# A trunk of four normalised sub-layers on one core: VectorE adds the squares of the first feed-forward's entry norms, token blocks 0 and 1

## The chip, the cores and the metric

The kernel runs on one core of a Trainium2 chip. The metric is the device time of one execution in microseconds (us), lower is better. The program is one launch that computes every output of the reference.

## The reference

One step of a two-layer trunk over 1024 prompt tokens and 8 x 16 sample tokens (1152 tokens together), model width 1024. Each layer is a mixer and a gated feed-forward, with an RMS norm before and after each:

```
def rms_norm(x, g):
    xf = x.astype(jnp.float32)
    y = xf * lax.rsqrt(jnp.mean(xf * xf, axis=-1, keepdims=True) + NORM_EPS)
    return (y * g.astype(jnp.float32)).astype(x.dtype)
...
        x = x + rms_norm(mix, g[1])
        f, fb = conv_ffn(rms_norm(x, g[2]), f_conv[layer], w['ffn_w_up'][layer], w['ffn_conv_w'][layer],
                         w['ffn_conv_b'][layer], w['ffn_w_down'][layer])
```

The case is about layer 0, between its mixer and its feed-forward: the mixer ends with `out = ag[..., :D_MODEL] * sigmoid(ag[..., D_MODEL:])` with `ag = z @ w_glu`, and then come the two norms above, `rms_norm(mix, g[1])` and `rms_norm(x, g[2])`.

## The kernel before

Features lie on the 128 partitions, in 8 tiles (`KD` = 8); the 1152 tokens lie along the free axis, in 3 blocks of 384 (`NB` = 3, `TB` = 384).

**The GLU steps.** `front` runs 24 steps, numbered k, block c = k // 8 and output tile m = k % 8. `Glu.tensor` computes in each step two halves, h = 0 (the gate) and h = 1 (the value), of 24 products of 128x384: a weight is split into a rounded head and the rest, and head times head, head times rest and rest times head are added (`products`). I call such a half a unit, numbered 2k + h. The weights of unit n are loaded by the SP queue into `w_raw` (`Weights.load`, which waits until the split of unit n - 2 is done), rounded by ScalarE into `w_head` (`Weights.round`, L836, which waits for the load and until TensorE is done with unit n - 2), and subtracted by VectorE into `w_rest` (`Weights.subtract`, L840). TensorE starts unit n when both are done. ScalarE then forms the sigmoid (L1617) and VectorE the product with it (L1623), which goes into `f`.

**The norms.** `Norm` handles six groups g = 0 to 5, two for each token block: group 2c is the norm of `f` for block c, group 2c + 1 the norm of x + norm(f). While the GLU steps of blocks 1 and 2 run, the groups 0 to 3 of blocks 0 and 1 run between them. In steps with m = 0 (even groups) and m = 4 (odd groups) ScalarE squares the block pair by pair, each pair 128x768 (two feature tiles), into three buffers `sq` (`Norm.squares`, L1423). The sum over the 1024 features is made by TensorE after the step with m = 1 or m = 5 (`Norm.sums`, L1433): for each of the four pairs, two tiles by three token columns of 128, six products of 128x128 with a matrix of ones, so 24 a group. ScalarE takes the root (`roots`, L1441), VectorE the inverse and widens it (`inverse`), TensorE spreads it over the partitions after the next step (`spread`, L1457), and VectorE scales (`scale`, L1486, and the addition to x, L1482) in the steps m = 2 and 3, or 6 and 7. As there are three buffers and four pairs, the fourth square has to wait until the first pair has been summed; ScalarE's program has it in the step m = 1 or 5:

```
                for h in range(2):
                    if c and m in (0, 4):
                        norm1.squares(act, g + m // 4, 2 * h, h + 2, glu.free, KD * (c - 1))
                    if c and m in (1, 5) and h == 1:
                        norm1.squares(act, g + m // 4, 3, 4, glu.free, KD * (c - 1))
                    if c and m == 7:
                        norm1.heads(act, c - 1, 2 * h, 2 * h + 2)
                    w.round(act, 2 * k + 2 + h, h)
```

Groups 4 and 5 (block 2) come after the last GLU step, among the first units of the feed-forward. GpSimd issues the loads and stores of x (its own DMA queue) and computes `x_rest` of blocks 0 and 1 (`Norm.rest`, L1462).

The order of each engine's instructions is that of the written program; nothing is scheduled by costs. Between engines only semaphores order the work. Buffer numbers in the names (`sq_182`) are those of the built program.

Of the kernel before, what the change touches and what calls it, by code (L numbers as in the profile page):

```python
# [20 lines left out]
P = 128  # L21
D = 1024
KD = D // P
# [1355 lines left out]
class Norm:  # L1379


    def __init__(self, env, f, x_dram, post, pre, h_head, h_rest, x, sq, wide, small):
# [7 lines left out]
        self.scaled, self.renewed, self.headed = (sem(n) for n in ("scaled", "renewed", "headed"))  # L1390

    TT, HALF = TB // P, KD // 2
# [18 lines left out]
    def squares(self, act, g, k0, k1, ready=None, at=0):  # L1411

        c, r = self.place(g)
        for k in range(k0, k1):
            n = self.HALF * g + k
            if n >= 3:
                act.wait_ge(self.summed, n - 2)
            if r == 1:
                act.wait_ge(self.renewed, self.HALF * c + k + 1)
            else:  # L1420
                act.wait_ge(ready, at + 2 * k + 2)
            src = self.pair(self.f, k, c) if r == 0 else self.x[c][:, 2 * k:2 * k + 2, :]
            act.activation(self.sq[n % 3][:, :, :], src, ACT.Square).then_inc(self.squared, 1)  # L1423

    def sums(self, pe, g):
        for k in range(self.HALF):
            n = self.HALF * g + k
            pe.wait_ge(self.squared, n + 1)
            if g and k == 0:
                pe.wait_ge(self.rooted, g)  # L1430
            for h in range(2):
                for j in range(self.TT):
                    m = pe.matmul(self.env.bank[6][:, P * j:P * j + P], self.sq[n % 3][:, h, P * j:P * j + P], self.env.ones[:, :],  # L1433
                                  start=(k == 0 and h == 0 and j == 0), stop=(k == self.HALF - 1 and h == 1), skip_group_check=True)
            m.then_inc(self.summed, 1)

    def roots(self, act, g):
        act.wait_ge(self.summed, self.HALF * g + self.HALF)
        if g >= 2:
# [622 lines left out]
def front(env, i, x_head, x_rest, x_res, m_par, gates, tails, m_tails, xm_d, xc_d, sz_d):  # L2062
# [20 lines left out]
    norm1 = Norm(env, f, x_res, 1, 2, x_head, x_rest, [xs[0], xs[1], xs[0]], [two(f"sq{k}", A0 + 24576 + 3072 * k) for k in range(3)],  # L2083
                 wides(A0 + 33792), small)
    ys = [big("y_even", A1), big("y_odd", U0)]
# [14 lines left out]
    with nc.Block() as block:  # L2100
# [124 lines left out]
        def _(act):  # L2225
            w.round(act, 0, 0, first=True)
            w.round(act, 1, 1, first=True)
            for k in range(steps):
# [1333 lines left out]
```

## Time and profile before

| what | value |
|---|---|
| time, median of 3 runs | 3905.59 us (3903.67 to 3906.49) |
| the profiled execution | span 3903.4 us; its own time is not listed apart from the three above |
| instructions of the span | 53745 |
| TensorE busy | 3481.6 us, 89% of the span |
| VectorE busy | 1908.1 us, 49% |
| ScalarE busy | 1149.8 us, 29% |
| GpSimd busy | 511.1 us, 13% |
| mean granted TensorE clock | 0.935 of full |
| GLU steps 8 to 23, during which groups 0 to 3 run | about 360.8 to 524.4 us of the span |

The span runs from the first to the last instruction, the time is that of the whole execution. PE is TensorE, PEld its weight load, DVE VectorE, ACT ScalarE, POOL GpSimd. A PE instruction's duration reaches from its start to its end in the pipeline, so that the durations of consecutive ones overlap; what one costs is seen in the distance between two starts. A product of two float32 operands with the ones stands in the trace as two PE instructions (48 for the 24 products of a group). "<-issue" ahead of a PE instruction means that the profile shows no other engine that released it at that time.

### The profile page before, as it was taken

The numbers are of one execution on the slowest core, as the hardware profiler recorded it, in microseconds if no ns is written. First come the engines' busy times: TensorE is split into PE (matmuls) and PEld (weight loads), VectorE is DVE, ScalarE is ACT, GpSimd is POOL, SyncE is SP. The second block draws the span as 40 slices with busy tenths as digits, with TensorE's granted clock in tenths as the row PEclk, the third lists the DMA queues.
The fourth block names the chain that finished last, engine by engine and source line by source line (L and its number), as shares of the span: only waits on it lengthen the run. The fifth ranks groups of instructions, "written<-read, shape, count | busy, mean of one in ns | idle before, by whom it ended". The sixth has DMA issues, their size and how long they took to land. (4 is left out here: it accounts for less than half of the span.)

```text
span 3903.4 us, 53745 instructions
## 1 busy us (share of the span) xinstructions
PE 3481.6 (89%) x20489; PEld 3262.9 (84%) x20489; DVE 1908.1 (49%) x2953; ACT 1149.8 (29%) x1880; POOL 511.1 (13%) x769
## 2 busy tenths in 40 slices
PE   5549989999999989999478779997995999999997
PEld 4449989999999989999344468887985999999996
DVE  8933554445444563222533346664655544454455
ACT  5233343332333232222222212222112323323321
POOL 2240111000000120000120032221001100000000
PEclk8679999999999999999678789998997999999998
DMA  3444431111111123332399632222122111111112
GB/s 78 140 121 137 134 96 44 39 44 44 39 44 44 57 101 120 106 104 94 84 262 297 214 92 81 75 67 76 38 71 75 44 39 44 44 41 42 44 38 101
DMA packets 366303, 337.08 MB, mean 86 GB/s; under 512 B 42888, under 2 KB 294024, under 8 KB 365956
## 3 DMA queue, kind: packets, MB, share of 16 engines
q1 hardware_dynamic: 345318, 288.49, 24.1%
q0 software_dynamic: 13600, 38.24, 3.7%
q10 hardware_dynamic: 7176, 7.35, 0.6%
q8 instruction: 157, 2.57, 0.3%
q14 instruction: 52, 0.43, 0.0%
HBM read 231.12 MB, written 100.53 MB: 85 GB/s over the span
## 5 line engine op out<-in xcount | busy, mean ns | idle before, releaser
L1583 PE MATMUL pair<-x_head,w_head 128*128 128x384 f32 x1488 | 505.6, 340 | 53.0 <-DVE w_rest L840 30.4
L1583 PE MATMUL pair<-x_rest,w_head 128*128 128x384 f32 x1488 | 502.5, 338 | 0.0
L1583 PE MATMUL pair<-x_head,w_rest 128*128 128x384 f32 x1488 | 502.1, 337 | 0.0
L840 DVE TENSOR_TENSOR w_rest<-w_raw,w_head 128x1024 fp32r<-128x1024 f32 x228 | 291.9, 1281 | 414.4 <-ACT w_head L836 414.3
L836 ACT ACTIVATE w_head<-w_raw 128x1024 fp32r<-128x1024 f32 x228 | 242.4, 1063 | 686.8 <-PE pair L856 166.9
L1238 PE MATMUL pair<-x_head,w_head 128*128 128x384 f32 x1056 | 354.0, 335 | 10.5 <-DVE w_rest L840 7.5
L1238 PE MATMUL pair<-x_rest,w_head 128*128 128x384 f32 x1056 | 353.5, 335 | 0.0
L1238 PE MATMUL pair<-x_head,w_rest 128*128 128x384 f32 x1056 | 353.5, 335 | 0.0
L1583 PEld LDWEIGHTS pair<-x_head,w_head 128*128 128x128 f32 x1488 | 283.5, 191 | 58.0 <-issue 52.5
L1328 DVE SCALAR_TENSOR_TENSOR cv<-u,par,cv 128x1024 f32<-128x1024 f32 x88 | 112.8, 1282 | 358.5 <-ACT u L1294 358.5
L1583 PEld LDWEIGHTS pair<-x_rest,w_head 128*128 128x128 f32 x1488 | 283.5, 191 | 0.0
L1583 PEld LDWEIGHTS pair<-x_head,w_rest 128*128 128x128 f32 x1488 | 283.3, 190 | 0.0
L1851 DVE SCALAR_TENSOR_TENSOR cv<-u,par,cv 128x1024 f32<-128x1024 f32 x88 | 112.8, 1282 | 340.4 <-ACT u L1792 340.4
L1238 PEld LDWEIGHTS pair<-x_head,w_head 128*128 128x128 f32 x1056 | 198.9, 188 | 11.5 <-issue 7.5
L1238 PEld LDWEIGHTS pair<-x_rest,w_head 128*128 128x128 f32 x1056 | 198.8, 188 | 0.0
L1238 PEld LDWEIGHTS pair<-x_head,w_rest 128*128 128x128 f32 x1056 | 198.8, 188 | 0.0
L1753 PE MATMUL pair<-a_head,w_head 128*128 128x384 f32 x528 | 179.9, 341 | 2.2 <-DVE f L1882 0.9
L1289 ACT ACTIVATE cv<-pair,par 128x384 f32<-128x384 f32 x132 | 88.5, 670 | 315.5 <-PE pair L1238 304.5
L1259 PE MATMUL pair<-a_head,w_head 128*128 128x384 f32 x528 | 179.3, 340 | 1.5 <-DVE f L1355 0.4
L1753 PE MATMUL pair<-a_rest,w_head 128*128 128x384 f32 x528 | 177.5, 336 | 0.0
L1753 PE MATMUL pair<-a_head,w_rest 128*128 128x384 f32 x528 | 177.5, 336 | 0.0
L1259 PE MATMUL pair<-a_head,w_rest 128*128 128x384 f32 x528 | 177.5, 336 | 0.0
(510 smaller groups left out, 6982.0 us busy)
## 6 DMA issues: line engine op xcount, KB each, us to landing
w_raw<-in_ffn_w_up_dram SPq DMA_DIRECT2D x88, 512.0 KB, 3.9
hs<-in_state_mlstm_C_dram SPq DMA_DIRECT2D x52, 512.0 KB, 6.6
out_dram<-hs SPq DMA_DIRECT2D x52, 512.0 KB, 4.5
w_raw<-in_s_w_glu_dram SPq DMA_DIRECT2D x48, 512.0 KB, 4.1
w_raw<-in_ffn_w_down_dram SPq DMA_DIRECT2D x44, 512.0 KB, 3.7
w_raw<-in_mlstm_w_up_dram SPq DMA_DIRECT2D x32, 512.0 KB, 4.3
xm_d<-xm SPq DMA_DIRECT2D x16, 576.0 KB, 3.9
xc_d<-xc SPq DMA_DIRECT2D x16, 576.0 KB, 2.8
```

The source lines that it names most:

```text
L836: act.activation(self.head[slot][:, :], self.raw[slot][:, :], ACT.Copy).then_inc(self.rounded, 1)
L840: dve.tensor_tensor(self.rest[slot][:, :], self.raw[slot][:, :], self.head[slot][:, :].bitcast(F32), ALU.subtract).then_inc(self.split, 1)
L1238: m = pe.matmul(banks[k % 2][c][:, 0:TB], lhs[k % 2][:, P * i:P * i + P], rhs[:, i, TB * c:TB * c + TB], start=(i == 0 and q == 0), stop=( ...
L1259: ins = pe.matmul(banks[m % 2][c][:, 0:TB], lhs[m // 4][:, cols], rhs[s][:, k, TB * c:TB * c + TB], start=(k == 0 and q == 0), stop=(k == ...
L1289: act.activation(cv[g][:, TB * c:TB * c + TB], bk[c][:, 0:TB], ACT.Identity, scale=at(par, t, TAP + H, TAP + H + 1), bias=at(par, t, BIAS, ...
L1328: ins = dve.scalar_tensor_tensor(out=cp, in0=up[:, j:j + SEQ], scalar=tw, in1=cp, op0=ALU.mult, op1=ALU.add)
L1583: m = pe.matmul(out[:, 0:TB], lhs[slot][:, P * k:P * k + P], rhs[:, k, TB * c:TB * c + TB], start=(k == 0 and q == 0), stop=(k == KD - 1 a ...
L1753: ins = pe.matmul(out[:, 0:TB], lhs[m // 4][:, cols], rhs[s][:, k, TB * c:TB * c + TB], start=(k == 0 and q == 0), stop=(k == 1 and q == 2))
L1851: ins = dve.scalar_tensor_tensor(out=cp, in0=up[:, j:j + SEQ], scalar=tw, in1=cp, op0=ALU.mult, op1=ALU.add)
```

## The change

`Norm` gets an argument `gathers`, the number of groups handled in the new way; the first feed-forward's entry norms (`norm1`) get 4, so groups 0 to 3, and all other norms keep 0. In such a group VectorE adds the second, third and fourth square pair to the first (`gather`, three additions of 128x768), and TensorE multiplies only the sum with the ones: one pair, six products. All four squares now come in the step m = 0 or 4. The fourth goes into the buffer of the second, and therefore waits until VectorE has added the second.

```
+    def slot(self, g, k):
+        return self.sq[(g + (0, 1, 2, 1)[k]) % 3 if g < self.gathers else (self.HALF * g + k) % 3]
...
+    def gather(self, dve, g, k0, k1):
+        for k in range(k0, k1):
+            dve.wait_ge(self.squared, self.HALF * g + k + 1)
+            if k > 1:
+                dve.wait_ge(self.gathered, 3 * g + k - 1)
+            dve.tensor_tensor(self.slot(g, 0)[:, :, :], self.slot(g, 0)[:, :, :], self.slot(g, k)[:, :, :], ALU.add).then_inc(self.gathered, 1)
...
@@ squares @@
-            if n >= 3:
-                act.wait_ge(self.summed, n - 2)
+            if g < self.gathers:
+                if g and k == 0:
+                    act.wait_ge(self.gathered, 3 * g)
+                if g and k == 2:
+                    act.wait_ge(self.summed, g)
+                if k == 3:
+                    act.wait_ge(self.gathered, 3 * g + 1)
...
@@ sums @@
-        for k in range(self.HALF):
-            n = self.HALF * g + k
-            pe.wait_ge(self.squared, n + 1)
+        parts = (0,) if g < self.gathers else range(self.HALF)
+        for k in parts:
+            if g < self.gathers:
+                pe.wait_ge(self.gathered, 3 * g + 3)
...
@@ front, scalar @@
                     if c and m in (0, 4):
-                        norm1.squares(act, g + m // 4, 2 * h, h + 2, glu.free, KD * (c - 1))
-                    if c and m in (1, 5) and h == 1:
-                        norm1.squares(act, g + m // 4, 3, 4, glu.free, KD * (c - 1))
+                        norm1.squares(act, g + m // 4, 2 * h, 2 * h + 2, glu.free, KD * (c - 1))
...
@@ front, vector @@
+                if c and m in (1, 5):
+                    norm1.gather(dve, g + m // 4, 2, 4)
                 w.subtract(dve, 2 * k + 2, 0)
+                if c and m in (0, 4):
+                    norm1.gather(dve, g + m // 4, 1, 2)
```

How this stands in the programs. First ScalarE, steps 20 and 21 (block 2, m = 4 and 5, group 3), before: L1617 is the sigmoid, `w_head` the rounding of a unit's weights, `sq` a square, L1441 the root.

```order
L1617 ACTIVATE gate_170<-pair 128x384
L1423 ACTIVATE sq_182_2458<-x_odd_2457 128x768
L1423 ACTIVATE sq_183_2459<-x_odd_2457 128x768
L836 ACTIVATE w_head_150<-w_raw_148 128x1024
L1423 ACTIVATE sq_184_2460<-x_odd_2457 128x768
L836 ACTIVATE w_head_151<-w_raw_149 128x1024
L1617 ACTIVATE gate_171<-pair 128x384
L836 ACTIVATE w_head_150<-w_raw_148 128x1024
L1423 ACTIVATE sq_182_2458<-x_odd_2457 128x768
L836 ACTIVATE w_head_151<-w_raw_149 128x1024
L1441 ACT_TABLE_LOAD
```

The same place of the changed program.

```order
L1648 ACTIVATE gate_170<-pair 128x384
L1433 ACTIVATE sq_182_2458<-x_odd_2457 128x768
L1433 ACTIVATE sq_183_2459<-x_odd_2457 128x768
L836 ACTIVATE w_head_150<-w_raw_148 128x1024
L1433 ACTIVATE sq_184_2460<-x_odd_2457 128x768
L1433 ACTIVATE sq_183_2459<-x_odd_2457 128x768
L836 ACTIVATE w_head_151<-w_raw_149 128x1024
L1648 ACTIVATE gate_171<-pair 128x384
L836 ACTIVATE w_head_150<-w_raw_148 128x1024
L836 ACTIVATE w_head_151<-w_raw_149 128x1024
L1472 ACT_TABLE_LOAD
```

The fourth square has moved from the second step to the first, ahead of the rounding of the first step's second unit.

Next VectorE, steps 12 and 13 (block 1, m = 4 and 5, group 1), before: `w_rest` is the subtraction of a unit's weights, `f<-pair,gate` the product with the sigmoid, L1446 the inverse.

```order
L840 TENSOR_TENSOR w_rest_152<-w_raw_148,w_head_150 128x1024
L840 TENSOR_TENSOR w_rest_153<-w_raw_149,w_head_151 128x1024
L1623 TENSOR_TENSOR f<-pair,gate_170 128x384
L840 TENSOR_TENSOR w_rest_152<-w_raw_148,w_head_150 128x1024
L840 TENSOR_TENSOR w_rest_153<-w_raw_149,w_head_151 128x1024
L1623 TENSOR_TENSOR f<-pair,gate_171 128x384
L1446 RECIPROCAL small_166<-small_164 128x3
```

The same place of the changed program.

```order
L840 TENSOR_TENSOR w_rest_152<-w_raw_148,w_head_150 128x1024
L1451 TENSOR_TENSOR sq_183_2459<-sq_183_2459,sq_184_2460 128x768
L840 TENSOR_TENSOR w_rest_153<-w_raw_149,w_head_151 128x1024
L1654 TENSOR_TENSOR f<-pair,gate_170 128x384
L1451 TENSOR_TENSOR sq_183_2459<-sq_183_2459,sq_182_2458 128x768
L1451 TENSOR_TENSOR sq_183_2459<-sq_183_2459,sq_184_2460 128x768
L840 TENSOR_TENSOR w_rest_152<-w_raw_148,w_head_150 128x1024
L840 TENSOR_TENSOR w_rest_153<-w_raw_149,w_head_151 128x1024
L1654 TENSOR_TENSOR f<-pair,gate_171 128x384
L1477 RECIPROCAL small_166<-small_164 128x3
```

One addition (L1451) has come between the two subtractions of the first step, and two ahead of the first subtraction of the second.

## Rows read from the trace of the kernel before

**Rows 1.** The page: span, TensorE, and granted clock in 40 equal slices

```profile
span 3903.4 us, 53745 instructions
...
PE 3481.6 (89%) x20489; PEld 3262.9 (84%) x20489; DVE 1908.1 (49%) x2953; ACT 1149.8 (29%) x1880; POOL 511.1 (13%) x769
...
PEclk8679999999999999999678789998997999999998
```

**Rows 2.** Busy time by stretch, columns as in its first line

```profile
core 0: us, PE busy (x) PEld busy (x) DVE busy (x) ACT busy (x) POOL busy (x), PEclk, DMA share, GB/s
352.60:436.60 84.00, 83.37 (x516) 82.49 (x516) 38.25 (x53) 34.44 (x42) 5.71 (x8) 1.00 0.49 148
...
446.20:451.54 5.34, 0.01 (x1) 0.04 (x1) 5.34 (x2) 1.06 (x1) 4.14 (x3) 0.70 0.02 7
451.54:455.20 3.66, 3.66 (x12) 3.66 (x13) 1.50 (x2) 0.00 (x0) 0.74 (x1) 0.51 0.60 164
455.20:524.40 69.20, 68.83 (x434) 68.22 (x433) 29.85 (x40) 27.24 (x33) 4.36 (x6) 1.00 0.45 138
```

**Rows 3.** Waits, 352.6 to 524.4 us: total us, times, longest

```profile
PE pair L1583 <- issue: 6.8, 4, 5.3
...
ACT w_head L836 <- DMA w_raw<-in_s_w_glu_dram: 2.7, 1, 2.7
```

**Rows 4.** Timeline, PE, first sums: start, us, instruction

```profile
373.67 5.52 PE L1433 MATMUL pair<-ones,sq 128*128 128x128 f32 x48
378.95 0.42 PE L1583 MATMUL pair<-x_head,w_head 128*128 128x384 f32 x1
```

**Rows 5.** Busy time by stretch: sums of the second and fourth groups

```profile
413.62:418.89 5.27, 5.27 (x49) 5.27 (x49) 1.69 (x2) 3.07 (x3) 0.00 (x0) 1.00 0.34 97
...
501.55:506.82 5.27, 5.27 (x49) 5.27 (x49) 1.69 (x2) 3.07 (x3) 0.00 (x0) 1.00 0.33 98
```

**Rows 6.** Groups of instructions, 352.6 to 563 us

```profile
L1423 ACT ACTIVATE sq<-f 128x768 f32<-128x768 f32 x12 | 9.6, 836 | 12.1 <-PE pair L1433 12.1
...
L1482 DVE TENSOR_TENSOR x_even<-x_even,f 128x768 f32<-128x768 f32 x8 | 7.5, 954 | 0.0
```

**Rows 7.** Timeline, ACT, steps 8 and 9

```profile
360.98 0.49 ACT L1617 ACTIVATE gate<-pair 128x384 f32<-128x384 f32 x1 [3.07 <-PE pair L1583]
361.36 1.57 ACT L1423 ACTIVATE sq<-f 128x768 f32<-128x768 f32 x2
362.83 1.05 ACT L836 ACTIVATE w_head<-w_raw 128x1024 fp32r<-128x1024 f32 x1
363.78 0.84 ACT L1423 ACTIVATE sq<-f 128x768 f32<-128x768 f32 x1
365.20 1.06 ACT L836 ACTIVATE w_head<-w_raw 128x1024 fp32r<-128x1024 f32 x1 [0.58 <-PE pair L1583]
369.71 0.49 ACT L1617 ACTIVATE gate<-pair 128x384 f32<-128x384 f32 x1 [3.45 <-PE pair L1583]
...
375.21 0.84 ACT L1423 ACTIVATE sq<-f 128x768 f32<-128x768 f32 x1 [4.06 <-PE pair L1433]
```

**Rows 8.** Timeline, DVE, then PE, step 8

```profile
363.92 1.23 DVE L840 TENSOR_TENSOR w_rest<-w_raw,w_head 128x1024 fp32r<-128x1024 f32 x1 [4.28 <-ACT w_head L836]
...
364.76 0.34 PE L1583 MATMUL pair<-x_head,w_rest 128*128 128x384 f32 x1
365.24 0.41 PE L1583 MATMUL pair<-x_head,w_head 128*128 128x384 f32 x1
```

**Rows 9.** Timeline, DVE, POOL and PE, step 16

```profile
443.98 8.59 DVE L840 TENSOR_TENSOR w_rest<-w_raw,w_head 128x1024 fp32r<-128x1024 f32 x2 [1.82 <-ACT w_head L836]
...
443.19 7.15 POOL L1462 TENSOR_TENSOR x_rest<-f,x_head 128x768 fp32r<-128x768 f32 x4
...
451.54 0.66 PE L1583 MATMUL pair<-x_head,w_head 128*128 128x384 f32 x1 [5.34 <-issue]
```

**Rows 10.** DMA issues, 352 to 563 us: count, KB, us to landing

```profile
w_raw<-in_s_w_glu_dram SPq DMA_DIRECT2D x30, 512.0 KB, 4.0
```

More of the change, by code:

```diff
@@ L1379, with __init__ @@
 class Norm:
-    def __init__(self, env, f, x_dram, post, pre, h_head, h_rest, x, sq, wide, small):
+    def __init__(self, env, f, x_dram, post, pre, h_head, h_rest, x, sq, wide, small, gathers=0):
         self.env, self.f, self.x_dram, self.post, self.pre = env, f, x_dram, post, pre
@@ L1390, in __init__ @@
         self.scaled, self.renewed, self.headed = (sem(n) for n in ("scaled", "renewed", "headed"))
+        self.gathered, self.gathers = sem("gathered"), gathers
     TT, HALF = TB // P, KD // 2
@@ L1415, in squares @@
             n = self.HALF * g + k
-            if n >= 3:
-                act.wait_ge(self.summed, n - 2)
+            if g < self.gathers:
[5 more added lines that the diff above has]
+                    act.wait_ge(self.gathered, 3 * g + 1)
+            elif n >= 3:
+                if self.gathers:
+                    act.wait_ge(self.gathered, 3 * min(g, self.gathers))
+                act.wait_ge(self.summed, self.sums_of(g, k - 3) + 1)
             if r == 1:
@@ L1422, in squares, with sums_of @@
             src = self.pair(self.f, k, c) if r == 0 else self.x[c][:, 2 * k:2 * k + 2, :]
-            act.activation(self.sq[n % 3][:, :, :], src, ACT.Square).then_inc(self.squared, 1)
-    def sums(self, pe, g):
-        for k in range(self.HALF):
-            n = self.HALF * g + k
-            pe.wait_ge(self.squared, n + 1)
+            act.activation(self.slot(g, k)[:, :, :], src, ACT.Square).then_inc(self.squared, 1)
+    def slot(self, g, k):
+        return self.sq[(g + (0, 1, 2, 1)[k]) % 3 if g < self.gathers else (self.HALF * g + k) % 3]
+    def sums_of(self, g, k):
+        if k < 0:
+            g, k = g - 1, k + self.HALF
+        return g if g < self.gathers else self.gathers + self.HALF * (g - self.gathers) + k
+    def gather(self, dve, g, k0, k1):
[4 more added lines that the diff above has]
+            dve.tensor_tensor(self.slot(g, 0)[:, :, :], self.slot(g, 0)[:, :, :], self.slot(g, k)[:, :, :], ALU.add).then_inc(self.gathered, 1)
+    def sums(self, pe, g):
+        parts = (0,) if g < self.gathers else range(self.HALF)
+        for k in parts:
+            if g < self.gathers:
+                pe.wait_ge(self.gathered, 3 * g + 3)
+            else:
+                pe.wait_ge(self.squared, self.HALF * g + k + 1)
             if g and k == 0:
@@ L1432, in sums @@
                 for j in range(self.TT):
-                    m = pe.matmul(self.env.bank[6][:, P * j:P * j + P], self.sq[n % 3][:, h, P * j:P * j + P], self.env.ones[:, :],
-                                  start=(k == 0 and h == 0 and j == 0), stop=(k == self.HALF - 1 and h == 1), skip_group_check=True)
+                    m = pe.matmul(self.env.bank[6][:, P * j:P * j + P], self.slot(g, k)[:, h, P * j:P * j + P], self.env.ones[:, :],
+                                  start=(k == 0 and h == 0 and j == 0), stop=(k == parts[-1] and h == 1), skip_group_check=True)
             m.then_inc(self.summed, 1)
     def roots(self, act, g):
-        act.wait_ge(self.summed, self.HALF * g + self.HALF)
+        act.wait_ge(self.summed, self.sums_of(g, 0 if g < self.gathers else self.HALF - 1) + 1)
         if g >= 2:
@@ L2083, in front @@
     norm1 = Norm(env, f, x_res, 1, 2, x_head, x_rest, [xs[0], xs[1], xs[0]], [two(f"sq{k}", A0 + 24576 + 3072 * k) for k in range(3)],
-                 wides(A0 + 33792), small)
+                 wides(A0 + 33792), small, 4)
     ys = [big("y_even", A1), big("y_odd", U0)]
```

## The prediction

> **What bounds the kernel now.** I began with the page. TensorE is busy for 89% of the span [rows 1], so the question is whether it also sets the pace where this change works, in the GLU steps of blocks 1 and 2. The table by stretch answers that: from 352.6 to 436.6 us TensorE is busy for 83.37 of 84.00 us, from 455.2 to 524.4 us for 68.83 of 69.20 us, both at full granted clock, with VectorE and ScalarE busy for less than half of it [rows 2]. Between the two lies one large hole, 5.34 us with TensorE idle and VectorE busy throughout, and behind it 3.66 us in which the granted clock is 0.51, the lower of the two levels (1.2 GHz) [rows 2]. The waits of the whole stretch say the same: TensorE waited 6.8 us in 4 pieces, of which 5.3 us are that hole, and the rounding of weights waited for its DMA only once, 2.7 us [rows 3]. So in this stretch everything that is taken from TensorE's queue shortens the run, as long as the other engines keep their dates.
>
> **What is removed.** The sums of the first group run from 373.67 us, the first start, to 378.95 us, when the next unit starts: 5.28 us for 48 instructions [rows 4]. The reader should look at distances of starts here and not at durations: one instruction takes longer than the distance, since they overlap. In the second and fourth groups the same stretch is 5.27 us each and full, with 48 of the 49 instructions in it being sums [rows 5]; the third (from 461.62 us) I read as the same. None of the four has a hole in it, although the fourth square is late in all of them: ScalarE starts it 4.06 us after its last work, at 375.21 us, released by the sum of the first pair [rows 7], and TensorE still has two pairs to sum then. So its lateness costs nothing now, and making it early gains nothing.
> 5.28 us / 48 = 0.110 us an instruction. 18 of 24 products go, which is 36 of 48 instructions: 36 x 0.110 = 3.96 us a group, and for four groups 15.84 us.
> The Trainium skill (TensorE: Matmul & The Clock Gate, section Back-to-back issue gap) gives about 81 ns as the sustained distance of products with 128 moving columns; that would make 144 x 0.081 = 11.7 us. The trace has the same thing at 0.110 us, and the same page's figure for loading 128 columns of weights (section LDWEIGHTS, columns over 1.2, so 107 ns) lies near it; the sum goes by the trace.
>
> **What is added.** Three additions of 128x768 a group on VectorE. The addition to x in the same stretch has this shape and also two inputs in SBUF: 0.954 us [rows 6]. 12 x 0.954 = 11.4 us of VectorE, which was busy for 38.25 of 84.00 us [rows 2]. On the path they cost something only where a unit's weights come late by them. There are two places.
> *First, step m = 0 or 4.* Behind the subtraction for unit 2k + 2 come one addition, then the fourth square, then the rounding and the subtraction for unit 2k + 3. Worked out for step 8: the subtraction starts at 363.92 and takes 1.23, so ends at 365.15, and TensorE starts unit 18 on it at 365.24 [rows 8]; this late start (0.31 us behind the 0.17 that belongs to a product, counted from 364.76) is there already and stays. Addition 365.15 + 0.95 = 366.10; fourth square 0.84 [rows 6] and 0.09 for the handover (that of 365.15 to 365.24) makes 367.03; rounding 1.06 [rows 7] makes 368.09; handover and subtraction 0.09 + 1.23 make 369.41; handover to TensorE 369.50. Instructions that follow each other on one engine overlap by about 0.1 us (two squares take 1.57 instead of 2 x 0.84, and the rounding starts at 362.83, before 361.36 + 1.57 = 362.93 [rows 7]); there are two such places (addition behind subtraction, rounding behind square), so about 369.3. The due date: ScalarE's rounding was released at 365.20, 0.44 behind the last start of unit 17 at 364.76 [rows 7, 8]; the sigmoid at 369.71 is released by the end of unit 18, whose last start is therefore at 369.27, and unit 19 could start 0.175 later ((369.27 - 365.24) / 23), at 369.45. So the new chain just makes it, by 0.15 us, or misses by 0.05 us. Before, this chain had 1.8 us in hand (rounding at 365.20 instead of some 367). I put it at 0, with 0.5 us a group as its bad end (handovers twice as long and an addition a third longer), 2 us together.
> The load for unit 2k + 5 also starts with that later subtraction: at about 369.4, landed 4.0 us later [rows 10] at 373.4. Its rounding is not possible before unit 19 is done, about 373.9, and unit 21 is due only after the 1.32 us of sums and unit 20, near 379. Even the worst landing that the rows suggest, that wait of 2.7 us for a DMA [rows 3], is hidden here, so 0.
> *Second, step m = 1 or 5.* Two additions stand ahead of the subtraction for unit 2k + 2. VectorE's product of step 8 follows the subtraction that ends at 369.3 (about 0.5 us, estimated as half of 0.954 for half the elements), the two additions end near 371.8, the subtraction near 373.1; unit 20 is due at 373.67 plus the 1.3 us of sums. The sums themselves need all additions by 373.67 [rows 4]: ready 1.9 us early. Cost 0. If the cover were gone, it would be the 1.9 us of two additions a group.
> The root, inverse and spreading now start up to 4 us earlier against the step that follows; nothing is late by that, and the spreading stands in TensorE's order after the next step anyway.
>
> **What stays.** The hole at 446.2 us: VectorE's subtraction started at 443.98 beside four GpSimd products that began at 443.19 and took 7.15 us; together with the next one it needed 8.59 us, and TensorE restarted at 451.54 us [rows 9]. GpSimd starts these products when step 15 is done, so they move with the rest and the hole keeps its size. The addition of group 2 comes behind the starved subtraction, when the products are over. It delays the weights of unit 35 by about 3 us, to about 455.7; unit 34 has the slow 3.66 us with 12 products in it [rows 2] and 12 more at 0.175, and ends near 457.3. The date holds by some 1.5 us. SP's queue has the same issues in the same order, as has GpSimd's.
>
> **The sum.** 3903.4 - 15.8 = 3887.6 us of span. The runs stand 0.3 to 3.1 us above that span, the median 2.2 us: 3905.6 - 15.8 = 3889.8 us, or -0.40%. What a measurement tells from no change is about 0.2%, 7.8 us.
>
> **Rivals.**
> *Given back at m = 0 and 4 (chance 0.06).* If squares or additions are slower than the rows, unit 2k + 3 starts late by as much. For it speaks that the slack is about 0.15 us; against it, that all durations in the chain are read from the same stretch. To give back half it needs 2 us a group: 4 x 2 = 8, so 3897.8 us, and within 0.2% from there up.
> *TensorE isn't the bound at the joints (0.04).* The gained time would stand as a longer hole, at 446 us or at the end of the last GLU step, and the time stay near 3905 us. Against it: both holes are timed from TensorE's own last steps through VectorE and GpSimd, and no DMA wait stands there except the 2.7 us.
> *Slower (0.03).* VectorE's addition, with two inputs in SBUF, is starved as the subtraction was [rows 9]. It would take 7.5 us in place of 0.95, hold the fourth square and the rounding, and TensorE would idle some 6.4 us a group and come back on half the clock as behind the hole, which costs 1.6 more (3.66 for 12 products that take 12 x 0.175 = 2.1 otherwise [rows 2]): 4 x 8.0 - 15.8 = 16 us more, 3921.8 us. It decides from holes of 4.3 us a group on, (15.8 + 7.8) / 4 = 5.9 less the 1.6. Against it: GpSimd's products stand in none of the four places but step 16, where they are over before.
> The Trainium skill (SBUF — State Buffer, section SBUF: two separate sides) has a rule for it: VectorE with two SBUF inputs and a GpSimd instruction that reads SBUF take a shared pair of ports as an exclusive lock, and the later one blocks fully. The trace agrees with it in step 16 (7.15 us of products, a subtraction held for about as long).
> *More (0.05).* If in step 16 the subtraction came ahead of the products, or TensorE kept its clock, the 5.3 us and 1.6 us would go: 3889.8 - 6.9 = 3882.9 us. The lead of 0.8 us that the products had speaks against it.
> *As forecast (0.82):* 3889.8 us, own range 3887 to 3893 (1.5 us of scatter between runs on either side, and up to 2 us of the first place).
>
> **How the numbers follow.** Faster by over 0.2%: forecast, more, and a third of the first rival, 0.89. Within 0.2%: the rest of it and the joints, 0.08. Slower 0.03. The range takes the forecast's own and goes up into the first rival, to 3896; below to 3886.
>
> **What would show it.** In the changed profile the sums should be 12 instructions a group in 1.32 us; TensorE's busy share there as high as before; the additions 0.95 us each; no wait of the sums for them; the rounding behind the fourth square starting some 1.8 us later than before, and TensorE's start of unit 2k + 3 at most 0.1 us late. The step from the start of step 8 to 524.4 us should be 15.8 us shorter, and everything behind unchanged. I am wrong if holes of over 0.5 us stand at those starts, if an addition takes over 2 us, or if the hole in step 16 changes.

## The result

The changed kernel takes 3886.49 us, median of 4 runs (3881.45 to 3889.08); the kernel before took 3905.49 us beside it (3903.67 to 3906.49, 4 runs). The ratio is 0.995, 95% interval 0.9937 to 0.9962: 19.0 us less, where 15.8 were forecast. The page of the changed kernel:

```profile
span 3883.2 us, 53474 instructions
...
PE 3468.4 (89%) x20345; PEld 3251.5 (84%) x20345; DVE 1917.9 (49%) x2965; ACT 1150.5 (30%) x1880; POOL 509.5 (13%) x769
...
PEclk7679999999999999999678789998997999999998
```

Against [rows 1], TensorE has 144 instructions fewer, the number forecast, and is busy 13.2 us less; the span is 20.2 us shorter. VectorE has its 12 additions. Four stretches of the GLU steps, in busy time by stretch (the first sums; the stretch with the hole of step 16; the half-clock stretch behind it; most of what follows):

```profile
core 0: us, PE busy (x) PEld busy (x) DVE busy (x) ACT busy (x) POOL busy (x), PEclk, DMA share, GB/s
...
373.47:374.72 1.25, 1.25 (x13) 1.25 (x13) 0.00 (x0) 0.99 (x1) 0.00 (x0) 1.00 0.62 166
436.00:443.24 7.24, 1.95 (x13) 1.66 (x11) 7.24 (x2) 0.43 (x1) 6.04 (x4) 0.91 0.22 81
443.24:448.50 5.26, 5.26 (x17) 5.26 (x17) 3.32 (x4) 1.79 (x2) 0.39 (x1) 0.50 0.39 108
451.19:509.00 57.81, 57.35 (x343) 56.74 (x341) 32.35 (x43) 25.53 (x31) 4.36 (x6) 1.00 0.50 154
```

The sums take 1.25 us where they took 5.28 [rows 4]. TensorE stays full and at full clock (2.4 GHz, 1.00) around them. The hole still stands (last rows of this section), and the half-clock stretch behind it (0.50, 1.2 GHz) lasts 5.26 us, not 3.66 [rows 2]. TensorE's waits in the GLU steps are as they were, 6.8 us in 4 pieces [rows 3]:

```profile
engine line waited for: us in total, times, longest us
PE pair L1614 <- issue: 6.8, 4, 5.3
```

Now the chain that the prediction timed in step 8: the timeline of ScalarE, of VectorE, and of TensorE around the hole (start, us, instruction, idle time ahead of it and its releaser).

```profile
363.61 0.84 ACT L1433 ACTIVATE sq<-f 128x768 f32<-128x768 f32 x1
365.87 0.85 ACT L1433 ACTIVATE sq<-f 128x768 f32<-128x768 f32 x1 [1.43 <-DVE sq L1451]
366.62 1.04 ACT L836 ACTIVATE w_head<-w_raw 128x1024 fp32r<-128x1024 f32 x1
...
364.89 0.95 DVE L1451 TENSOR_TENSOR sq<-sq,sq 128x768 f32<-128x768 f32 x1
367.70 1.23 DVE L840 TENSOR_TENSOR w_rest<-w_raw,w_head 128x1024 fp32r<-128x1024 f32 x1 [1.86 <-ACT w_head L836]
368.84 0.55 DVE L1654 TENSOR_TENSOR f<-pair,gate 128x384 f32<-128x384 f32 x1
369.31 2.01 DVE L1451 TENSOR_TENSOR sq<-sq,sq 128x768 f32<-128x768 f32 x2
371.24 1.22 DVE L840 TENSOR_TENSOR w_rest<-w_raw,w_head 128x1024 fp32r<-128x1024 f32 x1
...
437.61 0.34 PE L1614 MATMUL pair<-x_head,w_rest 128*128 128x384 f32 x1
443.24 0.66 PE L1614 MATMUL pair<-x_head,w_head 128*128 128x384 f32 x1 [5.29 <-issue]
```

The fourth square waits for the first addition, the rounding follows it, and the subtraction ends at 368.93. Unit 18's last product starts at 369.13 and unit 19's first would start 0.17 later: the chain makes it by 0.3 us. The hole of step 16 is 5.63 us between starts.

The starts of TensorE's other products, set side by side for the two traces, show where the time went. The stretch from 352.6 to 524.2 us (times of before), the GLU steps, is 15.35 us shorter; from there to 563 us 1.32 more are gained, in the mLSTM stage (1862 to 2918 us) 2.27, behind it 2.37 are lost, and in the second feed-forward's loop (3050 to 3836 us) 3.70 are gained. That last stretch holds the same code in both kernels. This is where the excess over the forecast had to be looked for.

### The profile page after: what moved, and what is told of

Same layout as the page of the kernel before. It is cut to its first block and busy times, and to the rows that moved or that the text cites. A ratio compares the mean times of both kernels' runs of the same rounds, so it can differ in the third digit from the quotient of the medians.

```text
span 3883.2 us, 53474 instructions
## 1 busy us (share of the span) xinstructions
PE 3468.4 (89%) x20345; PEld 3251.5 (84%) x20345; DVE 1917.9 (49%) x2965; ACT 1150.5 (30%) x1880; POOL 509.5 (13%) x769
## 3 DMA queue, kind: packets, MB, share of 16 engines
q10 hardware_dynamic: 7176, 7.35, 0.6%
## 5 line engine op out<-in xcount | busy, mean ns | idle before, releaser
L1784 PE MATMUL pair<-a_head,w_rest 128*128 128x384 f32 x528 | 177.5, 336 | 0.0
L1784 PE MATMUL pair<-a_rest,w_head 128*128 128x384 f32 x528 | 177.5, 336 | 0.0
L1259 PE MATMUL pair<-a_rest,w_head 128*128 128x384 f32 x528 | 177.5, 336 | 0.0
```

What stands on the lines that cost most here:

```text
L1259: ins = pe.matmul(banks[m % 2][c][:, 0:TB], lhs[m // 4][:, cols], rhs[s][:, k, TB * c:TB * c + TB], start=(k == 0 and q == 0), stop=(k == ...
L1784: ins = pe.matmul(out[:, 0:TB], lhs[m // 4][:, cols], rhs[s][:, k, TB * c:TB * c + TB], start=(k == 0 and q == 0), stop=(k == 1 and q == 2))
```

## The experiments

Times are medians, with the range and the number of runs, the ratio against the kernel before on the same chip, and its 95% interval. The experiments ran in four batches. The kernel before had 3907.34 us (3900.78 to 3915.1, 21 runs) in the first batch, 3909.59 in the second, 3905.38 in the third and 3906.83 in the fourth.

### 1. The two kernels again

No edit. 

> The kernel before once more, nothing changed. In its first trace TensorE pauses for 1.37, 1.29 and 1.35 us at the three points where the loop of the second feed-forward starts its next round (3278.91, 3431.06 and 3583.13 us); the changed kernel has none of the three and that is where about 3.6 us of its unforecast gain lie. If these pauses belong to the program (where its instructions lie), this trace has the same three. If they come and go from execution to execution, it has another number of them, and the 3.6 us are scatter and no effect of the change.

> The changed kernel once more, nothing changed. If the pauses belong to the program, none of over 1 us stands at the loop edges of the second feed-forward, and the time is 19 us below before. If they are scatter, some appear, and the ratio over more rounds moves towards the 15.8 us of my sum (0.9959). The first four times lay between 3881.45 and 3889.08 us, so more rounds should also tell whether this scatter of 7.6 us, which before did not have (2.8 us), stays.

Before: 3907.21 us (3903.97 to 3911.43, 10), 1.0003 (0.9993 to 1.0012). After: 3886.24 us (3884.42 to 3891.24, 5), 0.9952 (0.9938 to 0.9966). The spans were 3908.1 and 3882.7, so two executions of before differ by 4.7 us; the mLSTM stage alone made 3.06 of it. Between the two of before the GLU steps differ by 1.0 us: the half-clock stretch behind the hole lasts 3.7 us in one and 5.9 us in the other. In both of after they are 15.35 us shorter than in the first of before, so 16.4 us shorter than in the second.

### 2. The products alone, TensorE still waiting for all four squares

```
         for k in range(self.HALF):
             n = self.HALF * g + k
             pe.wait_ge(self.squared, n + 1)
...
+            if k and g < self.short:
+                continue
...
```

The second, third and fourth square pair of groups 0 to 3 are left out of the sum, and VectorE adds nothing.

> The kernel before, but in groups 0 to 3 only the first square pair is multiplied with the ones (6 products a group, as in the changed kernel) and nothing is added by VectorE; the other three pairs are left out of the sum, so the norms of blocks 0 and 1 are those of a quarter of the features. My sum: 4 x 4.0 = 16 us less in the GLU steps, the whole gain of the change. Rival: if part of the gain came from moving the fourth square or from VectorE's work, this one gains less than the changed kernel there. As it has the same number of TensorE instructions as the changed kernel, it should also lack the pauses at the loop edges if these depend on where the instructions lie.

3891.82 us (3887.3 to 3895.39, 4), 0.996 (0.9945 to 0.9975). Only 2.7 us a group were gained, 9.7 us in the GLU steps. TensorE's waits in the GLU steps say why:

```profile
PE pair L1586 <- issue: 6.8, 4, 5.3
PE pair L1586 <- ACT sq L1424: 4.4, 4, 1.2
```

Each of the four groups waits 1.1 to 1.2 us for its fourth square. With 24 products the two pairs still to be summed covered it; with 6 nothing does. So once the sums are short the wait for the late fourth square costs 1.3 us a group (2.7 us gained in place of 4.0): 5.5 us of the GLU steps against experiment 3, of which the profile shows 4.4 us as waiting.

### 3. The products alone, without the wait

```
-        for k in range(self.HALF):
+        parts = (0,) if g < self.short else range(self.HALF)
+        for k in parts:
...
```

The same pairs are left out of the sum, but TensorE no longer waits for their squares.

> As the run with products left out and no additions (the norms of blocks 0 and 1 are again those of a quarter of the features: only the first square pair of groups 0 to 3 is summed), but TensorE no longer waits for the other three square pairs before it goes on. In that run TensorE waited 1.25 us a group for the fourth square, which ScalarE can only start once the first pair is summed, and the groups gained 2.7 us each in place of 4.0. Theory: without this wait it gains the 4.0 us a group of the changed kernel, 16.1 us in the GLU steps, so the additions cost nothing and the early fourth square is what makes the small sums possible without a wait. Rival: it gains less or more than the changed kernel there; then the additions, or the chain behind them, cost or gain the difference.

3884.42 us in one execution, span 3882.7. The GLU steps are shorter by 8.07 and 7.35 us in their two blocks, with the full change by 8.15 and 7.35. The additions and the chain through the fourth square cost nothing that can be seen.

### 4. The additions alone

Three additions of the same shape at the same places on VectorE, into a buffer that nobody reads; squares and sums as before.

```
...
+            dve.tensor_tensor(self.scratch[:, :, :], src, src, ALU.add).then_inc(self.extras, 1)
...
+                if c and m in (1, 5):
+                    norm1.extra(dve, g + m // 4, 2, 4)
                 w.subtract(dve, 2 * k + 2, 0)
+                if c and m in (0, 4):
+                    norm1.extra(dve, g + m // 4, 1, 2)
```

> The kernel before with its 24 products a group, and on VectorE 12 additions of 128x768 with two inputs in SBUF at the places where the changed kernel has them, into a scratch tile that nobody reads. My sum puts their cost at 0: the time is that of before within 2 us, and no pause of TensorE grows. Rival: if VectorE's additions delay weights, TensorE starts a unit of steps 8, 12, 16 or 20 later, by up to 1 us each. It has all TensorE instructions of before, so the pauses at the loop edges should be there if they depend on the place of TensorE's instructions alone.

3905.5 us (3898.91 to 3912.1, 10), 0.9998 (0.9987 to 1.0008). No stretch of the GLU steps moved by more than 0.06 us.

### 5. One more addition in the chain

```
                 if c and m in (0, 4):
+                    norm1.extra(dve, g + m // 4, 0, 1)
                     norm1.gather(dve, g + m // 4, 1, 2)
```

> The changed kernel with one more addition of 128x768 (into a scratch tile) on VectorE in the steps m = 0 and 4, ahead of the addition that the fourth square waits for, so that the chain to the weights of unit 2k + 3 is about 0.9 us longer. My prediction gave this chain 0.15 us to spare in step 8. In the changed kernel no pause is seen at unit 2k + 3, in step 8 VectorE's subtraction ended at 368.93 us and the unit was due at about 369.3: 0.3 us to spare. So I expect TensorE to start unit 2k + 3 late by 0.5 to 0.7 us in steps 8, 0.3 to 0.6 us in 12 and 20, and not at all in step 16 (whose unit before runs at half the clock): 1.5 to 2 us together. Rival: the chain has more to spare than worked out, and no pause appears.

3880.94 us in one execution, span 3879.2; the whole time says nothing here, since the stages behind it scattered by more than the effect (the mLSTM stage was 5.5 us shorter than in before). The timeline of TensorE at the start of unit 19 does:

```profile
369.15 0.34 PE L1623 MATMUL pair<-x_head,w_rest 128*128 128x384 f32 x1
369.91 0.41 PE L1623 MATMUL pair<-x_head,w_head 128*128 128x384 f32 x1 [0.42 <-issue]
```

A distance of 0.76 us where 0.17 is normal, so 0.59 us lost, against an addition of 0.95: 0.3 to 0.4 us were in hand in step 8. Steps 12 and 20 lose 0.37 each, so they had 0.5 to 0.6 in hand, and step 16 loses nothing: 1.3 us in all.

### 6. GpSimd's products out of the way of the subtraction

```
-            for k in range(KD // 2):
+            pool.wait_ge(w.split, 37)
+            for k in range(2):
+                norm1.rest(pool, 0, k)
+            pool.wait_ge(glu.free, 18)
+            for k in range(2, 4):
                 norm1.rest(pool, 0, k)
```

The four products for block 0 come two by two, each pair behind a subtraction and not beside it.

> The changed kernel, but GpSimd's four products x_rest of block 0 no longer start when step 15 is done: two wait until VectorE has subtracted the weights of unit 36, two until the product of step 17. This is the hole of step 16, which my prediction took as staying. If GpSimd's products starve VectorE's subtraction (as the rows say), the hole of 5.5 us and the stretch at half the clock behind it go: 6.9 us less than the changed kernel, about 3880 us. Rival: the subtraction was slow for another reason (its weights' load), and the hole stays; or the products now starve another subtraction, and a hole of the same size stands one or two steps later.

3879.09 us (3873.99 to 3886.58, 4), 0.9927 (0.9906 to 0.9947). GpSimd's and VectorE's timelines:

```profile
444.72 3.63 POOL L1493 TENSOR_TENSOR x_rest<-f,x_head 128x768 fp32r<-128x768 f32 x2 [10.02 <-DVE w_rest L840]
449.99 3.65 POOL L1493 TENSOR_TENSOR x_rest<-f,x_head 128x768 fp32r<-128x768 f32 x2 [1.64 <-DVE f L1654]
...
435.53 1.23 DVE L840 TENSOR_TENSOR w_rest<-w_raw,w_head 128x1024 fp32r<-128x1024 f32 x1 [1.83 <-ACT w_head L836]
436.67 0.95 DVE L1451 TENSOR_TENSOR sq<-sq,sq 128x768 f32<-128x768 f32 x1
439.48 1.23 DVE L840 TENSOR_TENSOR w_rest<-w_raw,w_head 128x1024 fp32r<-128x1024 f32 x1 [1.86 <-ACT w_head L836]
```

The subtractions of step 16 take 1.23 us each (8.59 for two before [rows 9]), TensorE runs from 433.58 to 445.72 us without a pause, and the GLU steps are 8.0 us shorter than in after: the hole and the slow clock behind it. The Trainium skill (SBUF — State Buffer, section SBUF: two separate sides) calls the pair of ports that VectorE and GpSimd share an exclusive lock, and the trace agrees: the starvation goes when the two engines' work is apart.

Together with the last GLU step: the product with the sigmoid goes ahead of the scaling, and GpSimd's products for block 1 wait for the last split.

```
+            pool.wait_ge(w.split, 2 * steps + 2)
...
+                if k == steps - 1:
+                    glu.vector(dve, k)
...
                 if k < steps - 1:
                     w.subtract(dve, 2 * k + 3, 1)
-                glu.vector(dve, k)
+                    glu.vector(dve, k)
```

> The kernel with GpSimd's products of block 0 later, once more, with more rounds: 8 us less than the changed kernel in the GLU steps, so a ratio to before of about 0.9930 (the first time 0.9927, 0.9906 to 0.9947).

> The same, and two moves at the joint of the last GLU step: VectorE makes the product of step 23 (which TensorE waits 3.0 us for) ahead of the second half of group 3's scaling, and GpSimd's products of block 1 wait for the weights of unit 49. Theory from the rows: TensorE's pause of 3.35 us at that joint shrinks to about 1 us, the slow clock that sometimes follows it stays away, and the delayed subtraction (8.2 us beside GpSimd's products) is no longer needed by a TensorE that comes earlier: 2 to 4 us less than without. Rival: the heads of block 1 and the squares of group 4 come later by the product and the gain is lost at the sums of group 4.

rest_later2: 3880.38 us (3871.99 to 3882.78, 5), 0.9927 (0.9914 to 0.9941). joint: 3874.65 us (3873.92 to 3881.53, 5), 0.9923 (0.9909 to 0.9936). The pause at the last step fell from 3.35 us between starts to 1.03, 2.3 us less; the intervals don't tell the two kernels apart. By its interval joint is faster than the changed kernel (0.9937 to 0.9962); those of rest_later and rest_later2 overlap it, and their 8.0 us are read from the GLU steps alone.

### 7. Where the rest came from: pauses at the loops' back edges

Each feed-forward is a loop in the program, with three back edges 152 us apart. TensorE's timeline of the kernel before at the first one of the second loop:

```profile
3278.73 0.34 PE L1259 MATMUL pair<-a_rest,w_head 128*128 128x384 f32 x1
3278.91 0.34 PE L1259 MATMUL pair<-a_head,w_rest 128*128 128x384 f32 x1
3280.28 0.43 PE L1238 MATMUL pair<-x_head,w_head 128*128 128x384 f32 x1 [1.03 <-DVE f L1355]
```

And of the changed kernel, with VectorE's addition at L1355 behind it:

```profile
3261.93 0.34 PE L1259 MATMUL pair<-a_head,w_rest 128*128 128x384 f32 x1
3262.11 0.34 PE L1238 MATMUL pair<-x_head,w_head 128*128 128x384 f32 x1
...
3262.31 0.56 DVE L1355 TENSOR_TENSOR f<-f,pair 128x384 f32<-128x384 f32 x1 [0.48 <-PE pair L1259]
```

1.37 us before, 0.17 after, at the same place. The releaser that the first row names is misleading: in the second fence TensorE goes on before that addition has started. What differs is a queue that carries instructions. The page's row of it (packets, MB, share), in the kernel before:

```profile
q8 instruction: 157, 2.57, 0.3%
```

In the changed kernel:

```profile
q8 instruction: 129, 2.11, 0.2%
```

In after_pad16 (the changed kernel with 16 transposes ahead, below):

```profile
q8 instruction: 156, 2.56, 0.3%
```

In before_pad112 (the kernel before with 112 of them):

```profile
q8 instruction: 122, 2.00, 0.2%
```

A packet is 2.57 MB / 157 = 16.4 KB. From 3281 to 3583 us (two rounds) the kernel before shows 17 of them, the changed one in its two rounds none at all.

Edge by edge the two go together. The 18 traces of this case have 108 back edges. Of the rounds that begin with a pause (75) each has 8 to 10 packets, counted from 8 us ahead of its first product; of those that begin without (33) none has any. At every paused edge one packet starts 2.7 to 3.4 us ahead of the round's first product, and the next 0.3 to 0.9 us behind it.

The theory: TensorE's program is fetched in blocks, and where the loop lies against the blocks decides whether the back edge finds its block there. The change has removed 288 instructions of TensorE (a product is a weight load and a matmul) ahead of both loops. The test puts tiny transposes, two instructions each, ahead of the GLU steps:

```
             for k in range(16):
+                pe.transpose(env.bank[7][:, 0:8], env.ident[0:8, :], env.ident[0:8, 0:8])
```

with 16 or 78 in after, 112 in before, and 8 to 120 in rest_later. The Trainium skill (Advanced Engine Details and Errata, section ISA Cache) gives 16 KB and 256 instructions for a line of the instruction cache, which agrees with 16.4 KB a packet; by it the loop's place modulo 256 counts. That section gives no price for a fetch at a loop's back edge. A round of the second loop is 1829 instructions of TensorE in the trace (864 products, their weight loads, 101 of the sequencer), so 7.1 blocks of 256.

> The changed kernel with 16 small transposes (32 TensorE instructions) ahead of its first GLU product, where TensorE waits 28 us for weights anyway; their result is not read. The traces so far: the queue 'instruction' of the DMA moves blocks of 16 KB; the loop of the second feed-forward fetches 17 of them in two rounds of before and pauses at the start of each round, and fetches none in the changed kernel. Theory: what decides is where the loop begins within such blocks. Between before and after TensorE's program is 288 instructions shorter; if a block holds 256 (16 KB at 64 B, an estimate from the block size), that is the same place but for 32, and these 32 are put back here. Then the pauses are back: 6 of 6 loop edges of the two feed-forwards with 0.7 to 1.8 us each, and the time is 3 to 5 us above the changed kernel. Rival: the number of instructions or chance decides, and it behaves like the changed kernel (1 to 3 pauses of 6).

> The changed kernel with 78 small transposes (156 instructions) at the hidden place. In the changed kernel the same program gave 3 and 2 pauses of 6 in two executions, so its place is at the border. Theory of the place: moved by 156 of 256 it is either clear of the border on the good side (0 pauses of 6, 2 us less than the changed kernel and less scatter) or on the bad one (6 of 6, 4 us more); a round is about 1820 TensorE instructions, 7.1 blocks, and touches 8 blocks from most places and 9 from few, so I expect the good side: 3884 us. Rival (chance): 1 to 3 pauses.

> The kernel before with 112 small transposes (224 TensorE instructions) at the same hidden place; with them the loops begin at the same place within a block of 256 as in the changed kernel (288 - 224 = 64, so not quite: 32 fewer are 224 more). Theory of the place: most of the six pauses go, though not one instruction of the norms has changed: 3 to 5 us less than before. Rival (the pauses belong to the number of instructions or to what the change does): 6 of 6 pauses and the time of before.

> The kernel with GpSimd's products later, and 112 small transposes (224 TensorE instructions) at the hidden place ahead of the GLU steps. Place of the feed-forwards' loops within blocks of 256 instructions: with before as 0, the changed kernel is at -32 (1 to 3 pauses of 6), 32 more instructions put it at 0 (6 of 6), 156 more at +124 (6 of 6), before with 224 more is at -32 (2 of 6). This one is at -64. Theory: the good side lies below -32 and this one has no pause and hardly any instruction block fetched in the loops; then 2 to 4 us less than rest_later (1.0 to 1.3 us for each pause gone, rest_later had 3). Rival: -32 is as good as it gets, and pauses come by chance.

> The same with 96 small transposes (192 instructions), so at -96. A round of the loop is about 1820 TensorE instructions, a little over 7 blocks of 256, so a loop that begins early in a block touches 8 blocks and one that begins late 9. Theory of the place: the good side is one contiguous stretch of places; no pauses here either if it is wider than 64, and 6 of 6 with fetches in every round if it ended between -64 and -96.

> The kernel with GpSimd's products later and 8 small transposes (16 instructions) ahead of the GLU steps, so its loops begin 16 instructions behind the changed kernel's place, at -16. If the good stretch is wider than 16 on this side, 0 to 3 pauses of 6, as at -32; if -32 is near its upper end, 6 of 6, as at 0.

> The same with 120 small transposes (240 instructions), at -48. They stand behind the barrier of the phase and cost about 5 us of their own, as the runs with 96 and 112 showed, so only the pauses count here. If the good stretch reaches down to -48, 0 to 3 pauses of 6, perhaps fewer than at -32; if -32 is its lower end, 6 of 6, as at -64.

What was measured, in order of the place (instructions ahead of the loops against before, modulo 256). A pause is the distance of starts at a back edge less the normal 0.17 us; there are six edges, and the last column is the sum of the pauses over them.

| kernel | place | time, us (range, runs) | ratio (interval) | q8 packets | edges with a pause | pauses, us |
|---|---|---|---|---|---|---|
| before | 0 | 3905.49 | 1 | 157 | 6 | 5.6 |
| again_before | 0 | see 1 | | 157 | 6 | 7.0 |
| dve_only | 0 | see 4 | | 157 | 6 | 6.3 |
| after_pad16 | 0 | 3888.52 (3885.87 to 3899.49, 6) | 0.9955 (0.9941 to 0.997) | 156 | 6 | 6.2 |
| rest_later_pad8 | -16 | 3881.89 (one run) | | 147 | 5 | 4.0 |
| pe_only | -24 | see 2 | | 111 | 1 | 0.7 |
| after | -32 | 3886.49 | 0.995 | 129 | 3 | 2.3 |
| again_after | -32 | see 1 | | 120 | 2 | 1.9 |
| pe_only2 | -32 | see 3 | | 120 | 2 | 2.4 |
| chain_longer | -32 | see 5 | | 120 | 2 | 2.1 |
| rest_later | -32 | see 6 | | 129 | 3 | 3.3 |
| rest_later2 | -32 | see 6 | | 129 | 3 | 2.9 |
| joint | -32 | see 6 | | 138 | 4 | 4.3 |
| before_pad112 | -32 | 3905.52 (3900.45 to 3914.78, 10) | 0.9997 (0.9987 to 1.0007) | 122 | 2 | 2.2 |
| rest_later_pad120 | -48 | 3909.88 (one run) | | 160 | 6 | 6.4, and 13.1 just behind |
| rest_later_pad112 | -64 | 3890.33 (3886.55 to 3896.12, 6) | 0.9959 (0.9946 to 0.9971) | 157 | 6 | 5.4, and 4.5 just behind |
| rest_later_pad96 | -96 | 3883.68 (3875.96 to 3890.7, 4) | 0.9944 (0.9922 to 0.9966) | 157 | 6 | 5.5 |
| after_pad78 | +124 | 3888.71 (3885.35 to 3892.04, 4) | 0.9948 (0.9931 to 0.9965) | 157 | 6 | 5.7 |

32 instructions put back in the changed kernel bring all six pauses back; 224 put into the kernel before (modulo 256 the same as 32 fewer) take four of the six away. The place decides, modulo 256, and not the change itself: at 0 both kernels pause six times, at -32 both fewer. (pe_only has eight semaphore instructions more than the changed kernel, so its place is -24.) But I had expected -64, -96 and +124 to be good places too, and they aren't: only -24, -32 and, barely, -16 are, and at -32 the number varies from 2 to 4 between executions.

Three more misses. The transposes are not hidden: in rest_later_pad96 they stand behind a barrier, 10.38 us of them:

```profile
274.24 10.38 PE L2202 MATMUL pair<-ident 8*128 8x8 f32 x96 [22.11 <-PEq L86]
```

In the three runs with 96 and 112 of them the GLU steps begin 3.7 to 5.1 us later than in the kernel before, which is why before_pad112 isn't faster than before. after_pad16 lost the pauses' 4 us in its span (16.1 us below before, after 20.2), but the ratios' intervals don't separate the two. And rest_later_pad120 had a span 28.8 us above that of rest_later, 7.9 of it ahead of the GLU steps (the transposes) and 7.4 and 12.4 in the two loops. Its timeline at the same edge shows what happens:

```profile
3272.61 0.34 PE L1259 MATMUL pair<-a_head,w_rest 128*128 128x384 f32 x1
3273.74 0.43 PE L1238 MATMUL pair<-x_head,w_head 128*128 128x384 f32 x1 [0.79 <-DVE f L1355]
3274.02 0.34 PE L1238 MATMUL pair<-x_rest,w_head 128*128 128x384 f32 x1
3274.19 0.34 PE L1238 MATMUL pair<-x_head,w_rest 128*128 128x384 f32 x1
3277.03 0.33 PE L1238 MATMUL pair<-x_head,w_head 128*128 128x384 f32 x1 [2.50 <-issue]
```

The pause at the edge, three products, and a second pause of 2.84 us between starts. All six edges have it, 2.1 to 2.8 us (in the first loop behind four products), and behind two of them some ten products start 0.32 us apart in place of 0.17. At -48, then, a block ends some 6 to 8 instructions behind the loop's first: the loop begins at about instruction 248 of a block (an estimate from these rows). The good place, 16 instructions further, is the one where it begins just behind a block's start (about 8), and before's is at about 40.

rest_later_pad112, at -64, bears this out. It too has a second pause at all six edges, 0.7 to 1.2 us between starts, behind 11 products in the second loop and 12 in the first:

```profile
3269.36 0.33 PE L1238 MATMUL pair<-x_rest,w_head 128*128 128x384 f32 x1
3270.52 0.33 PE L1238 MATMUL pair<-x_head,w_rest 128*128 128x384 f32 x1 [0.82 <-issue]
```

That is 8 products, 16 instructions, later than at -48, as blocks of a fixed length want it. In both kernels TensorE goes on 2.5 to 3.3 us behind the round's first product, wherever it stopped. So one block is fetched at the jump and the next behind it, and TensorE stops a second time where the first block is used up sooner than that. At -96 the first block lasts about 28 products, 4.8 us (an estimate), and there is no second pause. Why the pause at the edge itself is sometimes absent from 8, 16 and 24, and never from 40 on, stays open: a whole round can go by without a fetch, but what keeps it at hand there and not elsewhere no run shows.

## Why the prediction was right, and where it was wrong

**The step that failed** is the last one of the sum, "everything behind unchanged". The terms of the change itself came out within half a microsecond; outside the GLU steps 4.8 us more were gained, which the prediction had put at nothing without a row for it, and 3.4 us of them are pauses at loops' back edges.

**The bound: right.** What leaves TensorE's queue in the GLU steps leaves the run. pe_only2 shows it with nothing else changed.

**The removed sums: right, slightly short.** Forecast 0.110 us an instruction, 3.96 us a group. Measured 5.28 - 1.25 = 4.03 us a group, 16.1 for four. The Trainium skill (TensorE: Matmul & The Clock Gate, section Back-to-back issue gap) gives 81 ns; that would have made 11.7, and the trace does not agree with it here.

**The additions: right.** 12 at 0.95 us each, no cost by themselves (dve_only) and none in the change (pe_only2 against after).

**The chain at m = 0 and 4: right.** "Just makes it, by 0.15 us": by 0.3. The subtraction was forecast to end 5.49 us after the subtraction ahead of it started (363.92 to 369.41, less 0.1 for the overlaps); it took 5.19 (363.74 to 368.93). chain_longer confirms the slack from the other side.

**"Making it early gains nothing": right for 24 products, wrong for 6.** With short sums the late fourth square costs 1.3 us a group (pe_only). It didn't falsify the time, since the change moves the square too, but read as a price of that part it would have been wrong by 5.5 us.

**The hole "keeps its size": right, what is behind it not.** It is 5.63 us between starts. The half-clock stretch behind it grew from 3.66 to 5.26 us, which took back 0.8 us: the 17 instructions in it would take 3.0 us at full clock, so 2.3 us are lost there, where 12 in 3.66 lost 1.6. This is no effect of the change: the stretch lasts 5.9 us in again_before and 3.7 us in chain_longer. I had copied the duration of one execution instead of bounding it. That the GLU steps came out at 15.35 us is therefore luck to about a microsecond; against again_before it would be 16.4.

**The sum and "everything behind unchanged": this failed.** The GLU steps gave 16.1 - 0.8 = 15.3 us, the forecast within 0.5. The rest of the 20.2 us in the span came from behind: 3.4 us from pauses at back edges (5.6 to 2.3), 1.3 from the clock behind the last GLU step's pause, and 0.2 between stages that scatter. I had no row of a back edge in the prediction, and no rival for it. The 3.4 us come from the number of instructions that the change removes and not from what it computes (after_pad16 has it all and pauses six times); in the second pair of traces they are 5.1 (7.0 to 1.9). The 1.3 us are no effect of the change: again_after doesn't have them.

**The scatter was taken too small.** I gave 1.5 us on either side from three runs. With 21 runs the kernel before spans 14 us, and the profiled mLSTM stage moves from -5.7 to +5.3 us between kernels with the same code there. The median, 3886.49, lies below the forecast's own range of 3887 to 3893 and half a microsecond above the wider one's low end. By the intervals alone 15.8 us (0.996) can't be told from 19.0; only the traces show the excess.

**Rivals.** None of them came; GpSimd's starvation stayed in step 16, where "more" would have needed it gone. rest_later brought that about on purpose, and gave 8.0 us where 6.9 were worked out.

## What to carry to other kernels

Where the queue of the bounding engine is full, count the starts that leave it and time the longest chain that the moved work lengthens; both came out here within 0.3 us. Before a neighbour's lateness is called free, ask what covers it and whether the same change takes that cover away. And in a program with loops look at the engine's starts at each back edge, where a round jumps back to its first instruction: a change of instruction count ahead of a loop can move some microseconds that have nothing to do with its purpose, so compare stages with the same code before the whole time is credited to the change.

## What the runs showed of the hardware

- TensorE can pause at a loop's back edge, 0.7 to 1.8 us here, depending on where the loop lies modulo 256 instructions, and the profile puts it down to an engine that it doesn't wait for. The queue "q8 instruction" counts the fetches: 8 to 10 packets in a round behind a pause, none in a round without one. At two places a second pause follows, ended 2.5 to 3.3 us behind the round's first product; at the worse of them the pauses come to 19 us over six edges.
- Between executions of one kernel the stages' times scatter by several microseconds each, mostly in the mLSTM stage; its cause stays open.
- Behind the hole of step 16 (5.6 to 5.7 us between starts) TensorE runs at half clock for 3.7 to 5.9 us, in one and the same kernel too; behind the 3.35 us of the last GLU step for 0 to 5.9 us.
- Four GpSimd products (7.15 us) stop a VectorE subtraction of two SBUF inputs for as long as they run; the same products apart from it stop nothing.
